# The rests of the second block's early weights: from GpSimd to VectorE, with the rotations and the convolution placed between the chunks

## The reference, cut to what matters

```python
for l in range(DEPTH):                                # 2 layers
    h = rmsnorm_2(x, norm_g[l])
    proj = h @ w_in[l]                                # 1024 x (11 slices)
    q, k, v, ga, iq, ik, iw, xr, gr, ma, mb = jnp.split(proj, offsets, axis=-1)
    q = apply_rope(q, cos_a, sin_a); k = apply_rope(k, cos_a, sin_a)
    iq = apply_rope(iq, cos_i, sin_i); ik = apply_rope(ik, cos_i, sin_i)
    attn = dsa_attention(q, k, v, iq, ik, iw)         # indexer picks 64 keys
    xr = causal_depthwise_conv(xr, conv_w[l], conv_b[l])   # 4 taps, 1408 channels
    hr = rg_lru(xr, w_rg[l], b_rg[l], w_ig[l], b_ig[l], lru_lambda[l])
    ...
```

## Time and profile before

| | |
|---|---|
| runs of before | 2056.51, 2058.14, 2062.36 us; median 2058.14 |
| profiled execution: its time, its span | 2053.48 us, 2051.7 us |
| TensorE busy | 96% of the span (10292 matmuls) |
| VectorE, ScalarE, GpSimd busy | 38%, 26%, 13% |
| mean granted TensorE clock | 0.991 of full speed |
| first block | to 1259 us of the span |
| second block, layer 0 and layer 1 | 1259 to 1646 us, 1646 us to the end |

### The profile page before, as it was taken

The page is one execution under the profiler, slowest core; times in us unless marked ns, Lnnn a source line. Parts: engine busy times, 40 slices in busy tenths (PEclk is TensorE's granted clock), DMA queues, the critical chain, the costliest instruction groups (busy, mean ns, idle before and its releaser), DMA issues.

```text
span 2051.7 us, 25208 instructions
## 1 busy us (share of the span) xinstructions
PE 1977.1 (96%) x10292; PEld 1271.0 (62%) x10292; DVE 783.9 (38%) x1437; ACT 542.0 (26%) x1056; POOL 271.0 (13%) x244
## 2 busy tenths in 40 slices
PE   8999999999999989999999999999999999999997
PEld 6754444344446755443444445878789968877897
DVE  2332111111111322111111114578855645877655
ACT  2311010111101321110111102544355534442544
POOL 1300000000000300000000002972000057800000
PEclk9999999999999999999999999999999999999999
DMA  9346999999988246999999994452415834522253
GB/s 358 110 183 256 427 428 429 428 429 428 429 371 300 83 163 265 428 428 429 429 428 428 429 424 176 149 192 83 161 56 174 282 139 164 185 101 98 87 183 126
DMA packets 121312, 557.27 MB, mean 272 GB/s; under 512 B 4912, under 2 KB 49488, under 8 KB 96144
## 3 DMA queue, kind: packets, MB, share of 16 engines
q1 hardware_dynamic: 119664, 551.51, 67.7%
q10 hardware_dynamic: 1440, 4.36, 0.6%
q0 software_dynamic: 128, 0.30, 0.1%
HBM read 555.10 MB, written 1.05 MB: 271 GB/s over the span
## 4 chain that ended last, share of the span: by engine, by line
PE 83%; DVE 11%; ACT 3%; issue 2%; DMA 1%; POOL 0%; SPq 0%; POOLq 0%; DVEq 0%; ACTq 0%
PE bank L1880 11%; PE bank L1908 11%; PE bank L1882 11%; PE bank L1668 7%; PE bank L1676 6%; PE bank L1854 6%; PE bank L1660 4%; DVE work L1427 3%; PE bank L1979 3%; PE bank L1980 3%; PE bank L1981 3%; PE bank L1737 3%; PE bank L2056 3%; PE bank L2002 2%; PE bank L2001 2%; PE bank L2000 2%
## 5 line engine op out<-in xcount | busy, mean ns | idle before, releaser
L1349 DVE TENSOR_TENSOR work<-work,bank 64x512 f32<-64x512 f32 x64 | 67.3, 1052 | 411.7 <-ACT work L843 411.7
L1880 PE MATMUL bank<-ring,work 128*64 128x512 f32 x512 | 224.5, 594 | 0.0
L1882 PE MATMUL bank<-ring,work 128*64 128x512 f32 x512 | 224.4, 594 | 0.0
L1668 PE MATMUL bank<-hT,ring 128*128 128x256 f32 x992 | 223.1, 383 | 0.0
L707 POOL TENSOR_TENSOR w_lo<-ring,w_hi 128x512 fp32r<-128x512 f32 (+1 forms) x160 | 214.4, 1362 | 53.7 <-ACT w_hi L880 51.4
L665 POOL TENSOR_TENSOR stat<-stat,power 128x1 f32<-128x1 f32 (+1 forms) x18 | 10.8, 600 | 1579.8 <-DVE stat L1026 1544.6
L1668 PEld LDWEIGHTS bank<-hT,ring 128*128 128x128 f32 x992 | 188.7, 193 | 25.8 <-issue 0.7
L843 ACT ACTIVATE work<-bank 64x512 f32<-64x512 f32 x64 | 37.9, 592 | 544.3 <-PE bank L1882 544.3
L1540 DVE TENSOR_TENSOR w_lo<-ring,w_hi 128x512 fp32r<-128x512 f32 (+1 forms) x176 | 115.9, 678 | 79.5 <-ACT w_hi L976 79.2
L1676 PEld LDWEIGHTS bank<-work,h 128*128 128x128 f32 x1088 | 128.5, 192 | 19.8 <-issue 18.0
L1676 PE MATMUL bank<-work,h 128*128 128x128 f32 x1088 | 133.2, 276 | 1.5 <-DVE small L1307 1.5
(11 more groups left out here) (301 smaller groups left out, 3491.8 us busy)
## 6 DMA issues: line engine op xcount, KB each, us to landing
ring<-w_in_dram SPq DMA_DIRECT2D x34, 2048.0 KB, 8.7
ring<-w_gate_dram SPq DMA_DIRECT2D x32, 2048.0 KB, 12.9
ring<-w_up_dram SPq DMA_DIRECT2D x32, 2048.0 KB, 17.1
ring<-w_down_dram SPq DMA_DIRECT2D x32, 2048.0 KB, 18.7
ring_tail<-w_down_dram SPq DMA_DIRECT2D x16, 2048.0 KB, 19.2
work<-w_gate_dram SPq DMA_DIRECT2D x16, 2048.0 KB, 13.9
work<-w_up_dram SPq DMA_DIRECT2D x16, 2048.0 KB, 18.4
ring_tail<-w_gate_dram SPq DMA_DIRECT2D x16, 2048.0 KB, 14.2
```

The lines of the kernel that those rows point to most:

```text
L1349: dve.tensor_tensor(hid[up, b].rearrange("s (f p) -> s p f", f=FE), silu_g[up, b].rearrange(by_row, f=FE), m_bank(m)[up, :].rearrange(by_r ...
L1668: mm = pe.matmul(dst, w[:, k, f * P:(f + 1) * P], rhs[:, k], start=(k == 0), stop=(k == nk - 1))
L1880: pe.matmul(m_bank(m)[gate, :], lhs, wg[:, k], start=(k == 0), stop=(k == KD - 1), skip_group_check=True)
L1882: mu = pe.matmul(m_bank(m)[up, :], lhs, wu[:, k], start=(k == 0), stop=(k == KD - 1), skip_group_check=True)
```

## The change

GpSimd no longer makes the rests of pieces q = 0 to 9. VectorE makes them, with the same subtraction on the same operands. Each piece's rests are split four and four. Between the two halves VectorE does other work: for q = 0 to 4 two rotations, for q = 5 four rotations, for q = 6 the joining of the halves of xr 0 to 3, for q = 7 the convolution of tiles 0 to 3 and the joining of 4 to 7, for q = 8 the convolution of 4 to 7 and the joining of 8 to 10. The convolution of 8 to 10 stands behind the rests of q = 9. Within a group the convolution now goes tap by tap over the tiles, with one wait per tap in place of one per instruction. ScalarE's and TensorE's programs are as before.

```diff
@@ -698,14 +698,6 @@
             for layer in range(DEPTH):
                 inverse_rms(SECOND + layer)
 
-                for q in range(QPAIR):
-                    w = arrive2(pool, layer, SPLIT[q][0])
-                    for k in range(KD):
-                        g = chunk(layer, q, k)
-                        pool.wait_ge(chunk_hi, g + 1)
-                        n = w.shape[2]
-                        pool.tensor_tensor(w_lo[:, g % CHUNKS, 0:n], w[:, k], w_hi[:, g % CHUNKS, 0:n], ALU.subtract
-                                           ).then_inc(chunk_lo, 1)
             inverse_rms(FINAL)
 
 
@@ -1382,7 +1374,18 @@
                 dve.wait_ge(hT_hi_ready, layer + 1)
                 dve.tensor_tensor(hT_lo, hT[:], hT_hi, ALU.subtract).then_inc(hT_lo_ready, 1)
 
-                for c in range(14):
+                def rest_of_weights(q, k0, k1):
+
+                    w = arrive2(dve, layer, SPLIT[q][0])
+                    n = w.shape[2]
+                    for k in range(k0, k1):
+                        g = chunk(layer, q, k)
+                        dve.wait_ge(chunk_hi, g + 1)
+                        dve.tensor_tensor(w_lo[:, g % CHUNKS, 0:n], w[:, k], w_hi[:, g % CHUNKS, 0:n], ALU.subtract
+                                          ).then_inc(chunk_lo, 1)
+
+                def rotate(c):
+
                     name = ("rope", layer, c)
                     t = c % 2
                     full(dve, name)
@@ -1411,23 +1414,50 @@
                         S.settle()
                         S(dve.tensor_copy(roped[:, c % 4, ID:2 * ID], roped[:, c % 4, 0:ID]), roped2)
 
-                for j in range(RT):
-                    if j % 4 == 0:
-                        for jj in range(j, min(j + 4, RT)):
-
-                            name = ("xr", layer, jj)
-                            dve.wait_ge(xr_half, RT * layer + jj + 1)
-                            S.marks(dve.tensor_tensor(xr[:, jj, TAPS2 - 1:], xr[:, jj, TAPS2 - 1:], bank(name)[:, SEQ:],
-                                                      ALU.add), psum_read[TILE[name] % BANKS], uses(name))
-                        S.settle()
-                    S(dve.tensor_scalar(xc[:, j], xr[:, j, 0:SEQ], col(layer, "conv2", j), col(layer, "conv2_b", j),
-                                        ALU.mult, ALU.add))
+                rest_of_weights(0, 0, CHUNKS)
+                rotate(0)
+                rotate(1)
+                rest_of_weights(0, CHUNKS, KD)
+                for q in range(1, 5):
+                    rest_of_weights(q, 0, CHUNKS)
+                    rotate(2 * q)
+                    rotate(2 * q + 1)
+                    rest_of_weights(q, CHUNKS, KD)
+                rest_of_weights(QXR, 0, CHUNKS)
+                for c in range(10, 14):
+                    rotate(c)
+                rest_of_weights(QXR, CHUNKS, KD)
+
+                def join_halves(j0, j1):
+
+                    for j in range(j0, j1):
+                        name = ("xr", layer, j)
+                        dve.wait_ge(xr_half, RT * layer + j + 1)
+                        S.marks(dve.tensor_tensor(xr[:, j, TAPS2 - 1:], xr[:, j, TAPS2 - 1:], bank(name)[:, SEQ:],
+                                                  ALU.add), psum_read[TILE[name] % BANKS], uses(name))
+
+                def convolve(j0, j1):
+
+                    S.settle()
+                    for j in range(j0, j1):
+                        S(dve.tensor_scalar(xc[:, j], xr[:, j, 0:SEQ], col(layer, "conv2", j), col(layer, "conv2_b", j),
+                                            ALU.mult, ALU.add))
                     for tap in range(1, TAPS2):
                         S.settle()
-                        S(dve.scalar_tensor_tensor(out=xc[:, j], in0=xr[:, j, tap:tap + SEQ],
-                                                   scalar=col(layer, "conv2", tap * RT + j), in1=xc[:, j],
-                                                   op0=ALU.mult, op1=ALU.add),
-                          conv2_done if (j, tap) == (RT - 1, TAPS2 - 1) else None)
+                        for j in range(j0, j1):
+                            S(dve.scalar_tensor_tensor(out=xc[:, j], in0=xr[:, j, tap:tap + SEQ],
+                                                       scalar=col(layer, "conv2", tap * RT + j), in1=xc[:, j],
+                                                       op0=ALU.mult, op1=ALU.add),
+                              conv2_done if (j, tap) == (RT - 1, TAPS2 - 1) else None)
+
+                for q in range(3):
+                    rest_of_weights(QXR + q + 1, 0, CHUNKS)
+                    if q > 0:
+                        convolve(4 * q - 4, 4 * q)
+                    join_halves(4 * q, min(4 * q + 4, RT))
+                    rest_of_weights(QXR + q + 1, CHUNKS, KD)
+                rest_of_weights(QV + 1, 0, KD)
+                convolve(8, RT)
 
                 for j in range(12):
                     emptied(dve, ("dots", layer, j))
```

## The result

| | before | changed |
|---|---|---|
| median of its runs | 2059.37 us (4 runs) | 2073.81 us (2073.2 to 2075.54, 4 runs) |
| ratio, with 95% interval | | 1.0078 [1.0065, 1.0091] |
| the same, measured once more (5 runs) | | 1.0079 [1.0065, 1.0093] |
| profiled execution: span | 2051.7 us | 2071.2 us |
| GpSimd busy, VectorE busy | 271.0, 783.9 us | 56.6, 805.7 us |

The change makes the kernel slower by 0.78%, some 16 us by the ratio; the two medians of the table lie 14.4 us apart, inside the ratio's interval of 13.4 to 18.7 us. The forecast was 18.7 us more than before, 2076.8 us.

A forecast was written before the change was run, and what follows sets the result against it. It took TensorE, 83% of the chain, as the bound, with GpSimd following it. Layer 0 +7.9, layer 1 +6.65 and twice 1.2 + 0.9 us for rotations gave +18.7: 2058.1 + 18.7 = 2076.8 us, range 2062 to 2085.

The forecast's parts named there:

- rotations (q = 1 to 5): Per layer, TensorE late by 0.3 us at four fifth chunks (1.2 us) and 0.9 us before xr's first product.
- wait for the fifth rest of xr's third piece: TensorE finishes four chunks after 4.15 us; the fifth rest is ready at 9.8 us, so it waits 5.65 us.
- wait in v's first piece: TensorE has work for 5.45 us, the rest is ready at 9.9 us: 4.5 us of wait.
- third piece to gates: Sum from xr's third piece to TensorE's gates: 15.65 + 17.1 + 10.9 + 7.4 = 51.05 us, against 43.17 in layer 0.
- The deciding step: Convolution and joining between a piece's fourth and fifth rest, in xr and v, outlast TensorE's four buffered chunks.
- remainder: Time left for convolution and joining between the fourth and fifth rest: 2.35 us of the four slots' 4.15 us.
- rival 1: Freed VectorE pays: no TensorE wait for rests in xr and v, -8.4 us in all, 2049.7 us; chance 0.06.
- The block: Convolution of four tiles tap by tap on VectorE: 6.7 us, bounds 5.3 and 8.0 us.
- Rival 2: Waits or none, the convolution keeps one pace, 8.0 us for four tiles: +5.7 us, 2082.5 us; chance 0.10.
- The clock's term: Slow TensorE clock behind each wait in xr's third and v's first piece: 1.7 us, bounds 0 and 2.5.
- The level: Total of +18.7 us, counted from a profiled execution of 2053.48 us and added to the median 2058.1 us.
- Rival 3: All costs at their lower end, no clock loss, no wait at rotations: +2.1 us, 2060.2 us; chance 0.07.

The follow-up runs named there:

- half_taps: Changed kernel with the two middle convolution taps left out for tiles 0 to 7, so the result lacks them; 2055.55 us, ratio 0.9992 to the kernel before.
- tile_waits: Changed kernel with the convolution tile by tile and a wait before each tap, in the same places; 2079.81 us, ratio 1.0114 to the kernel before.
- spread_conv: Changed kernel with the convolution cut into units of two tiles and one tap, placed behind chunks' rests; 2046.23 us, ratio 0.9953 to the kernel before.
- after_again: Changed kernel measured once more, unaltered; 2074.23 us, ratio 1.0079 to the kernel before.
- rot_order: Changed kernel with the fourth rest of pieces 1 to 4 between the rotations, piece 5's behind its four; 2069.49 us, ratio 1.0058 to the kernel before.
- spread_all: Changed kernel with both the spread convolution and the fourth rest moved among the rotations; 2041.94 us, ratio 0.9932 to the kernel before.
- order_only: Changed kernel with the rests given back to GpSimd, VectorE keeping the new convolution order; 2053.95 us, ratio 0.9983 to the kernel before.

## Why the prediction was right, step by step

The steps of layer 0, from the starts in the trace:

| step | forecast | measured |
|---|---|---|
| rotations (q = 1 to 5), more than before | 2.1 us | 1.8 us |
| wait for the fifth rest of xr's third piece | 5.65 | 5.18 |
| xr's third piece, 1368.65 to 1384.10 | 15.65 | 15.45 |
| wait in v's first piece | 4.5 | 3.98 |
| v's first piece, 1384.10 to 1401.65 | 17.1 | 17.55 |
| v's second piece | 10.9 | 10.97 |
| first score to gates | 7.4 | 7.39 |
| third piece to gates | 51.05 | 51.36 |
| layer 0 as a whole, more than before | 10.0 | 10.3 |
| layer 1 as a whole, more than before | 8.75 | 7.5 |

- **The deciding step held.** Four slots cover four chunks, of which the fourth and the fifth rest take a part; VectorE's other work between these two rests costs what it exceeds the remainder by. half_taps and tile_waits move the block of convolution by -3.4 and +1.1 us, and the waits follow by -3.4 and +1.1 us each; spread_conv takes the block apart, and they vanish. The remainder comes out the same in the three kernels (layer 0, us, convolution and joining together):

| kernel | other work in xr's third piece, wait | remainder | other work in v's first piece, wait | remainder |
|---|---|---|---|---|
| half_taps | 4.32, 1.83 | 2.5 | 4.00, 0.59 | 3.4 |
| changed kernel | 7.75, 5.18 | 2.6 | 7.42, 3.98 | 3.4 |
| tile_waits | 8.87, 6.30 | 2.6 | 8.54, 5.12 | 3.4 |

The forecast, under rival 1, put it at 2.35 us for xr. It is clearly less than the 4.15 and 5.45 us that the four chunks last: the 4.0 us of half_taps in v fit into 5.45 and still cost a wait.

- **The block was 6.43 us, not 6.7.** Unwaited taps start 0.39 us apart and not 0.41 (two in 0.86 us at 0.47 us each, in spread_conv's rows). This made the fifth rest 0.3 us earlier than forecast. The rest of the 0.5 us in the waits is how they are counted: the profile counts from the end of the last matmul, the forecast from where the next one would have started. Rival 2's 8.0 us were out of reach even with a wait before each tap, 7.55 us.
- **The clock's term was right in size by luck.** In this execution it cost 1.7 us behind the first wait, as taken, and 2.5 us behind the second, which is the upper bound; with the shorter waits the errors nearly cancel. But the same two waits cost 1.6 to 2.9 us and 1.5 to 2.9 us in the two layers of after_again and rot_order, so that one profiled execution can lie 1 to 2 us per layer beside another.
- **The rotations** cost 0.24 us at a fifth chunk, not 0.3: one product of the changed kernel and the next rotation lie 12.03 us apart instead of 11.79. The bounds held it.
- **Layer 1 lost 1.2 us less than forecast.** To the attention it is 8.3 us (from layer 1's start to L2117, 238.1 us now and 229.8 before); another 0.8 us less come behind that, where the change has no instruction. It is the clock there: over the first 10 us behind the attention's wait of 5.0 us the granted clock is 0.77 in the kernel before and 0.85 in the changed one (rows below, in that order). Whether the change has a part in that, no run shows. In layer 0 xr's first two pieces take 0.4 us more than before and in layer 1 0.4 us less; the forecast had nothing for these.

```profile
1877.30:1887.30 10.00, 9.99 (x41) 8.61 (x42) 3.59 (x12) 3.22 (x11) 0.00 (x0) 0.77 0.01 2
...
1897.60:1907.60 10.00, 10.00 (x45) 8.76 (x46) 4.29 (x15) 3.22 (x11) 0.00 (x0) 0.85 0.01 2
```

- **The level was the weaker part.** The sum of 18.7 us was made against one profiled execution. Its like-for-like value is 17.8 us, the rest being in the first block; the ratios of the runs give 16.1 and 16.3 us, with intervals from 13.4 to 19.1 us. The profiled execution of before, 2053.48 us, was shorter than every other run of that kernel (the lowest of all is 2055.2), so a difference made against it may be a few microseconds too large; against it, after_again's two layers are 20.1 us longer, more than the 17.8 of the first. The sum is some 2 us above the ratios, within their intervals, and which of its terms these 2 us belong to stays open: the clock behind the waits alone moves by as much.
- **The rivals.** Rival 1 had the mechanism right that the rows suggested, and it is worth 10 us in spread_conv, near the rival's 8.4, and 14 us in spread_all, when the order lets it through; what stood against it, the cover of four chunks, was the whole of the answer. Rival 3 would have needed waits without a slow clock; in both executions of the changed kernel there is one behind each of them.

## What to carry to other kernels

When an engine takes over a step that feeds the critical engine, what counts is not its busy share but the longest piece of other work between two feedings. It is to be held against the work that lies buffered in front of the critical engine, less the time of the feedings themselves (here 2.6 of 4.15 us and 3.4 of 5.45 us were left). So cut the other work into units no longer than a feeding's slack and place one behind each: the same instructions then cost nothing, and waits between dependent ones are covered too. Measure an expected gain against the median of several executions, not against a profiled one alone, and compare the clock behind the waits before reading a difference of 1 or 2 us between two traces.

## What the runs showed of the hardware

- VectorE's instructions with two operands in SBUF take 0.48 to 0.50 us beside an idle GpSimd, and beside one that subtracts 1.0 us on average in order_only and up to 1.4 us; a block of 16 instructions (12 of these and 4 with one SBUF tensor and two columns) takes 6.43 and 18.7 us, nearly threefold. The joinings, with one operand in PSUM, take the same beside either.
- What the half clock costs behind a wait does not follow the wait's length, and differs between executions. Behind the waits of 5.2 us it cost 1.7 us in both layers of the changed kernel, 2.0 and 1.6 us in its second execution, 2.5 and 2.9 us in rot_order; behind those of 4.0 us 2.5 us in both layers, then 2.6 and 2.4, then 2.9 and 1.5. Behind 3.2 us it cost 1.7 us in the kernel before. In half_taps a wait of 1.8 us cost 1.7 us in layer 0 and 0.2 us in layer 1.
